# Post-norm multiply moved from VectorE to GpSimd, and the in-projection emitted in coarser steps, in an eight-core macaron transformer layer

## What is computed

```python
h = swiglu(rms_norm(x, ffn1_pre_g), w_gate1, w_up1, w_down1)      # hidden width 2816
x = x + 0.5 * rms_norm(h, ffn1_post_g)
h = hybrid_mixer(rms_norm(x, mix_pre_g), w_in, ..., w_out)        # 4 differential + 8 dilated heads
x = x + rms_norm(h, mix_post_g)
h = swiglu(rms_norm(x, ffn2_pre_g), w_gate2, w_up2, w_down2)
x = x + 0.5 * rms_norm(h, ffn2_post_g)
```

## Time and profile before

| | |
|---|---|
| median of three runs | 3164.24 us (3153.14 to 3166.34) |
| the profiled execution's own time | 3157.69 us |
| its span on the slowest core (core 2) | 3156.1 us |
| spans of the eight cores | 3124.6 to 3156.1 us |
| granted TensorE clock, mean by core | 0.972 to 0.979 |

### The profile page before, as it was taken

How to read it: one execution, slowest core, us unless ns; L and a number is a source line. 1 busy time by engine, 2 the same in 40 slices (tenths; PEclk the granted TensorE clock), 3 DMA queues, 4 the chain that set the end, 5 groups by cost and what they waited for, 6 DMA issues and landing times.

```text
span 3156.1 us, 59158 instructions; the slowest of 8 cores (3124.6 to 3156.1 us)
## 1 busy us (share of the span) xinstructions
PE 2850.2 (90%) x18494; PEld 1481.0 (47%) x18494; DVE 1606.8 (51%) x3054; ACT 1481.4 (47%) x2642; POOL 771.8 (24%) x1028
## 2 busy tenths in 40 slices
PE   6989889888999888999877889998999998999997
PEld 2434334345665544554333555664455543444443
DVE  4331641665554574553577555545655646640633
ACT  2313332355655665666552645565666655213112
POOL 1313334240122221002662000121000157114113
PEclk9999999999999999999999999999999999999998
DMA  7999986482353544224896412423211278735636
GB/s 143 171 180 220 221 209 195 140 242 65 76 150 91 120 99 75 58 66 119 242 241 192 112 34 64 122 70 99 73 50 51 79 222 253 217 97 180 184 94 177
DMA packets 189774, 433.52 MB, mean 137 GB/s; under 512 B 25024, under 2 KB 42688, under 8 KB 188864
## 3 DMA queue, kind: packets, MB, share of 16 engines
q0 software_dynamic: 64704, 218.67, 30.0%
q1 hardware_dynamic: 82048, 143.42, 16.5%
q10 hardware_dynamic: 42720, 67.65, 6.4%
HBM read 407.89 MB, written 99.09 MB: 161 GB/s over the span
## 4 chain that ended last, share of the span: by engine, by line
PE 69%; DVE 8%; DMA 8%; issue 7%; ACT 6%; POOL 1%; ACTq 1%; SPq 1%; DVEq 0%; POOLq 0%
PE ps L724 28%; PE ps L625 18%; PE ps L823 6%; PE ps L986 4%; PE ps L964 4%; PE ps L844 3%; PE ps L999 3%; PE ps L1022 2%; DMA xr<-x_s 2%; ACT qk L836 1%; DMA qk<-c_aug 1%; DVE sg L733 1%; DVE hT L738 1%; DMA x_s<-xr 1%; ACT Pt L1004 1%
## 5 line engine op out<-in xcount | busy, mean ns | idle before, releaser
L724 PE MATMUL ps<-xnh,wsl 128*128 128x512 bf16 x5632 | 1391.1, 384 | 92.2 <-DVE sg L733 20.2
L724 PEld LDWEIGHTS ps<-xnh,wsl 128*128 128x128 bf16 x5632 | 528.1, 99 | 660.3 <-issue 150.5
L625 PE MATMUL ps<-hT,wsl 128*128 128x512 bf16 x2816 | 672.0, 385 | 21.7 <-DMA wsl<-wd 14.8
L733 DVE SCALAR_TENSOR_TENSOR sg<-sg,ps 128x512 f32<-128x512 f32 x352 | 239.3, 685 | 445.6 <-ACT sg L731 414.3
L119 POOL DMA_DIRECT2D wsl<-wgu_s x286 | 155.2, 543 | 1218.0 <-PE ps L724 479.3
L971 ACT ACTIVATE Pt<-ps 128x512 bf16<-128x512 f32 x576 | 308.6, 580 | 280.5 <-PE ps L964 232.6
L625 PEld LDWEIGHTS ps<-hT,wsl 128*128 128x128 bf16 x2816 | 271.8, 99 | 323.1 <-issue 47.7
L473 POOL TENSOR_TENSOR rst<-rst,sq 128x512 f32<-128x512 f32 x276 | 345.4, 1261 | 313.6 <-ACT sq L471 309.4
L731 ACT ACTIVATE sg<-ps 128x512 f32<-128x512 f32 x352 | 207.8, 595 | 441.6 <-PE ps L724 370.5
L1004 ACT ACTIVATE Pt<-ps 128x512 bf16<-128x512 f32 (+3 forms) x640 | 325.0, 535 | 188.7 <-PE ps L999 101.9
L823 PE MATMUL ps<-xnf,winw 128*128 128x512 bf16 x1024 | 305.7, 384 | 22.1 <-ACT qk L836 9.1
(11 more groups left out here) (78 smaller groups left out, 2415.3 us busy)
## 6 DMA issues: line engine op xcount, KB each, us to landing
wsl<-wd_s POOLq DMA_DIRECT2D x232, 352.0 KB, 4.2
wsl<-wgu_s POOLq DMA_DIRECT2D x286, 256.0 KB, 3.6
xr<-x_s SPq DMA_DIRECT2D x256, 256.0 KB, 7.3
xr<-xT SPq DMA_DIRECT2D x164, 256.0 KB, 8.2
x_s<-xr ACTq DMA_DIRECT2D x128, 256.0 KB, 5.3
wsl<-wgu POOLq DMA_DIRECT2D x66, 256.0 KB, 7.0
outT<-xr ACTq DMA_DIRECT2D x64, 256.0 KB, 5.9
winw<-win POOLq DMA_DIRECT2D x48, 256.0 KB, 6.2
```

The source lines that it names most:

```text
L625: S.op(PE, lambda e, k=k, w_fn=w_fn, pb=pb: e.matmul(ps[pb][:], w_fn(k), rhs(k), start=(k == 0), stop=(k == nk - 1)), reads=w_bufs + [rhs_ ...
L724: S.op(PE, lambda e, wi=wi, pb=pb, kc=kc, tl=tl: e.matmul(ps[pb][:], wsl[wi][:, kc * 128:(kc + 1) * 128], xnh[:, kc, tl * TT:(tl + 1) * TT ...
L733: S.op(DVE, lambda e, tl=tl, pb=pb: e.scalar_tensor_tensor(sg[tl][:], sg[tl][:], 1.0, ps[pb][:], ALU.add, ALU.mult), reads=[B_sg[tl], B_ps ...
```

## The change

Three edits.

1. In `post`, the multiply of `ysb` by the inverse norm is issued on GpSimd. `scale(0)` and `scale(1)` stand ahead of the loop over the chunks, right after the fetch of x has been spawned; inside it, `scale(k + 2)` stands ahead of VectorE's addition of chunk k. VectorE keeps that addition (L599 before).
2. The planned delay after each chunk's addition is 1.3 instead of 1.45.
3. `tile_proj` yields after four large matmuls instead of two and after sixteen small ones instead of eight; `NSTEP` is 6 instead of 12. The planned time per projection is the same.

```diff
+                def scale(k):
+                    S.op(POOL, lambda e: e.tensor_tensor(ysb[:, k, :], ysb[:, k, :], rst[ry][:], ALU.mult),
+                         reads=B_ysb[k] + [B_rst[ry]], writes=B_ysb[k])
+
+                scale(0)
+                scale(1)
                 for k in range(NKC):
                     yield from landed(slots, k)
                     i = slots[k][0]
-                    S.op(DVE, lambda e, k=k: e.tensor_tensor(ysb[:, k, :], ysb[:, k, :], rst[ry][:], ALU.mult),
-                         reads=B_ysb[k] + [B_rst[ry]], writes=B_ysb[k])
+                    if k + 2 < NKC:
+                        scale(k + 2)
                     S.op(DVE, lambda e, k=k, i=i: e.scalar_tensor_tensor(
...
-                    yield ("d", 1.45)
+                    yield ("d", 1.3)
...
-                        if kc % 2 and kc < NKC - 1:
-                            yield ("c", 2 * PASS)
+                        if kc == 3:
+                            yield ("c", 4 * PASS)
...
                     G.give(pb)
-                    yield ("c", 2 * PASS)
+                    yield ("c", 4 * PASS)
...
-                    if tq < 3:
-                        yield ("c", NKC * SMALL)
+                    if tq == 1:
+                        yield ("c", 2 * NKC * SMALL)
...
-                yield ("c", NKC * SMALL)
-
-            NSTEP = 12
+                yield ("c", 2 * NKC * SMALL)
+
+            NSTEP = 6
```

## The result

The change makes the kernel slower. It takes 3247.14 us (median of four runs, 3243.77 to 3251.18), the kernel before, run beside it, 3158.69 us. The ratio is 1.029, 95% interval 1.0265 to 1.0315: 2.9%, 88 us. The forecast was 3165 us, range 3112 to 3218; the time lies outside it.

A forecast was written before the change was run, and what follows sets the result against it. The kernel was taken as bound by TensorE, with 306 us idle to win. Terms +22.5 - 16 - 8 + 1.9 = +0.4 us on the median of 3164.2 gave 3165 us, range 3112 to 3218.

The forecast's parts named there:

- the up to 10 us for the clock: Whole kernel: allowance within the forecast's bounds for a lower granted clock making idle time dearer, up to 10 us.
- (a): Out-projection, eight post-norms: GpSimd's added multiplies lengthen the two stretches by 10 and 12.5 us, together +22.5 us.
- a queue in order won't be fuller than some 95%: Out-projection: GpSimd's queue, also waiting for ScalarE's squares, fills at most some 95%, so stretches become 147 and 147.5 us.
- The rival with 0.25: Out-projection: GpSimd becomes the bound past some 90% busy; +47 - 10 - 4 + 2, with clock 45, 3209 us; chance 0.25.
- The multiply's price: All 24 post-norms: one multiply on GpSimd takes 1.157 us, as its add does, against 0.684 on VectorE; ends 1.14 and 1.71.
- The mutual hold-up: Post-norms: GpSimd and VectorE operations run one after the other; waiting adds nothing to 0.47 us per multiply, taken as 0.3.
- (b): First FFN, eight post-norms: VectorE's relief saves 2 us of idle time per post-norm, -16 us; ends -40 and +10.
- (c): Second FFN, eight post-norms: seven cost 0, the last, the tail, grows from 12.3 to 14.2 us, +1.9 us.
- The added wait: Second FFN: GpSimd's first multiply waits 1.95 us for ScalarE's inverse norm, ahead of weight loads and adds; priced at 0.
- My sign for this edit: In-projection: if waits for qk at L823 and L844 do not fall, the coarser steps are worth nothing.

The follow-up runs named there:

- the evenly paced kernel: The kernel before with only the six coarse in-projection steps, spread over the attention jobs as the twelve were: ratio 0.9970, 3140.6 us against 3149.3.

## Why the prediction was wrong

**What bounds the kernel** was read rightly, TensorE, and nearly three quarters of the loss is its idle time (63 of 88 us). That its busy time would stay was not: it grew by 24 us, for which the forecast had no term but the up to 10 us for the clock.

**(a), the out-projection**, had the right place and mechanism and failed in size. I gave +22.5 us; the multiply alone costs 27.3 + 21.5 = 48.8, twice as much. The term that failed is "a queue in order won't be fuller than some 95%": it is full at 78 to 81% of the stage. No row had given those 95%. I had set the added work against the stage's idle time. But the idle time stands between the post-norms, while GpSimd waits for the first squares or for a weight slot. Within one, from 1582 on, there was none left to fill. Of some 35 us added per stage (98 to 133 us busy), 11 found idle time and 24 didn't. The rival with 0.25 had this mechanism and this price, +47. Its point of decision, 90% busy, was never reached, and its -10 in the first FFN and -4 for edit 3 did not come.

**The multiply's price**: 1.275 us against the 1.157 taken from the add, so 10% more, within my ends. The rule of the Trainium skill ("GPSIMD Engine Reference", Engine selection), about twice VectorE's time or an estimated 1.37 us, is 7% above the run, which is at 1.86 times 0.684.

**The mutual hold-up** was seen and sized as alternating, at most one GpSimd operation per addition. It isn't bounded so: a VectorE operation can wait out several back to back, as here (GpSimd's operations during one addition of the changed kernel):

```profile
381.62 5.66 DVE L605 SCALAR_TENSOR_TENSOR xr<-ysb,gains,xr 128x512 f32<-128x512 f32 x1 [0.71 <-POOL ysb L595]
382.02 1.17 POOL L473 TENSOR_TENSOR rst<-rst,sq 128x512 f32<-128x512 f32 x1
383.13 1.27 POOL L595 TENSOR_TENSOR ysb<-ysb,rst 128x512 f32<-128x512 f32 x1
384.35 1.15 POOL L473 TENSOR_TENSOR rst<-rst,sq 128x512 f32<-128x512 f32 x1
385.46 1.26 POOL L595 TENSOR_TENSOR ysb<-ysb,rst 128x512 f32<-128x512 f32 x1
```

GpSimd's four operations follow each other without a pause (each is recorded as starting some 0.05 us before the one ahead ends). The addition, 0.74 us of work, starts ahead of the first of them and ends at 381.62 + 5.66 = 387.28, 0.56 us after the last (385.46 + 1.26 = 386.72). So semaphores are not the only coupling between these two engines' queues. The Trainium skill ("SBUF — State Buffer", Who interferes with whom) says, of VectorE's two-port mode, that whoever issues first has the shared ports for the whole instruction; for an addition with two SBUF inputs this trace shows another picture, since it started first and was held up by four in a row. By the comparison of multiplies and memsets the multiply's share of it is worth some 16 us of the time.

**(b), the first FFN**, -16 us, did not come. Its post-norms lie beside gate-up 1 to 4, where the multiply alone gives +5.5, +0.1, -5.2 and -3.8, some -3 in sum, and the kernel with the FFNs' multiplies alone is 1.0038. VectorE's relief is real: with one memset in place of the multiply these four stretches are 28 us shorter in sum, with three memsets 12 us. So GpSimd's load eats some 16 us of it here too, and the hold-up some 9. A case of both: an addition lasts from 328.5 to 334.1 beside four GpSimd operations, and at 340.1 a statistics matmul starts after 9.9 us of idle time, when VectorE has freed the bank and GpSimd has ended the last sum, both at 339.7. Before, no statistics matmul of a post-norm waited longer than 6.6 us.

**(c)** held: the tail is 13.7 us (3223.76 to 3237.46) against 12.3, +1.4 where +1.9 was given, and the last two jobs' gate-up stretches, with the post-norms under the full TensorE, are longer by 1 us at most; from the last gate-up result to the end it is 3.0 us in all. **The added wait** was nothing, as priced: TensorE waits 7.4 + 19.1 us for weights (`wgu_s` and `wd`) where it waited 9.4 + 14.8.

```profile
3223.76 12.49 POOL L595 TENSOR_TENSOR hT<-hT,rst 128x512 f32<-128x512 f32 x8 [2.25 <-ACT rst L462]
3225.19 12.27 DVE L605 SCALAR_TENSOR_TENSOR xr<-hT,gains,xr 128x512 f32<-128x512 f32 x8 [9.41 <-POOL hT L595]
```

**Edit 2** is nothing, as priced.

**Edit 3** failed in sign: -8 was given, +32 to +40 measured. I weighed the two halves of my argument wrongly. The longer time between giving a bank back and taking it is worth about 10 us, as the evenly paced kernel shows. The loss of the projection's matmuls in later jobs I had bounded at +20 and gave a chance of 0.06. I took the 9.9 us of waits at the scores as its measure. But that is what is left of a wait when something covers it, not what it is without cover: it doubled, and so did the epilogue's wait. And it was no measure of TensorE's busy time, which has 20 of the 32 us. My sign for this edit, that the waits for qk at L844 fall, came true for ScalarE (16.9 to 8.5 us) and said nothing on its worth.

## What to carry to other kernels

An engine's share of a stage says little on whether work fits in; count its operations between the event that starts a burst and the one that needs its end, and compare with that stretch alone. When a stream is cut into fewer pieces, check that whatever spreads the pieces still spreads them: a count rounded up to one per turn makes them come early. And a pair of VectorE and GpSimd operations that both read two SBUF tensors should not be priced one for one; the one can stand behind a whole run of the other.

## What was not expected of the hardware

A VectorE operation with two SBUF inputs, 0.74 us by itself, lasted 5.66 us beside four GpSimd operations in a row. The longest, 8.57 us from 2781.10 on, ran beside six multiplies: three pairs, from 2780.57, 2783.59 and 2786.62 on, with a weight load issued between the pairs. It ended 0.56 us after the last multiply; the 0.5 us without a multiply between two pairs, less than its own length, did not let it finish.

Memsets of GpSimd held it up nowhere: 740 to 753 ns in 56 instances. The Trainium skill ("SBUF — State Buffer", Who interferes with whom) says so too: a GpSimd instruction that only writes is no contender for such an operation.
